# Swapping the two copies of the turned probabilities between ScalarE and VectorE in the prompt attention

## The reference, cut to what matters

```
logits = q @ k^T * scale (+ a bias for fox and swa)
p = softmax(where(mask, logits, -1e30))
out = p @ v
```

## Time and profile before

| | |
|---|---|
| median of 3 runs | 2819.38 us (2811.65 to 2823.92) |
| the profiled execution's own time | 2807.96 us |
| its span, first to last instruction | 2806.0 us |
| mean granted TensorE clock, share of full speed | 0.989 |
| VectorE copies of chunks (L1736) | 144, all of 512 columns |
| ScalarE copies of chunks (L1312) | 144: 60 of 512 columns, 24 of 384, 36 of 256, 24 of 128 |
| first and last start of these copies | 244.8 to 1898.8 us |

### The profile page before, as it was taken

How to read it: one execution, slowest core, us unless ns; L and a number is a source line. 1 busy time by engine, 2 the same in 40 slices (tenths; PEclk the granted TensorE clock), 3 DMA queues, 4 the chain that set the end, 5 groups by cost and what they waited for, 6 DMA issues and landing times.

```text
span 2806.0 us, 39617 instructions
## 1 busy us (share of the span) xinstructions
PE 2695.5 (96%) x14966; PEld 2177.9 (78%) x14966; DVE 1698.6 (61%) x2196; ACT 1054.8 (38%) x1969; POOL 1050.4 (37%) x594
## 2 busy tenths in 40 slices
PE   8999999899999999999999999998999999999997
PEld 6986666787888887888879756667878888878886
DVE  4026777635564558778740377775355564688777
ACT  4225544423323332333332255554243233333333
POOL 1112000114545457767511210001146444667766
PEclk9999999999999999999999999999999999999999
DMA  4212001432333446444132200013413433654441
GB/s 145 63 29 61 25 18 44 137 135 98 124 139 126 150 173 251 142 138 134 61 115 64 66 24 17 17 50 131 163 70 139 157 118 140 238 195 143 143 142 75
DMA packets 164722, 308.75 MB, mean 110 GB/s; under 512 B 24720, under 2 KB 90416, under 8 KB 164592
## 3 DMA queue, kind: packets, MB, share of 16 engines
q1 hardware_dynamic: 161280, 303.59, 31.4%
q10 hardware_dynamic: 3312, 3.41, 0.4%
HBM read 207.40 MB, written 97.72 MB: 109 GB/s over the span
## 4 chain that ended last, share of the span: by engine, by line
PE 86%; DVE 8%; ACT 2%; issue 2%; POOL 1%; DMA 1%; SPq 0%; DVEq 0%; ACTq 0%; POOLq 0%
PE ps L2583 8%; PE ps L2587 8%; PE ps L2585 8%; PE ps L2493 7%; PE ps L2494 7%; PE ps L2495 7%; PE ps L2237 6%; PE ps L2104 6%; PE ps L2106 6%; PE ps L2105 6%; PE ps L2098 5%; PE ps L2310 3%; PE ps L2370 2%; PE ps L2204 1%; PE ps L2438 1%
## 5 line engine op out<-in xcount | busy, mean ns | idle before, releaser
L2583 PE MATMUL ps<-wq_hi,sa_hi 128*128 128x512 f32 x896 | 349.0, 390 | 5.3 <-DVE x L2034 5.3
L2587 PE MATMUL ps<-wq_hi,sa_lo 128*128 128x512 f32 x896 | 348.6, 389 | 0.0
L2585 PE MATMUL ps<-wq_lo,sa_hi 128*128 128x512 f32 x896 | 348.6, 389 | 0.0
L2034 DVE TENSOR_TENSOR x<-ps,x 128x1024 f32<-128x1024 f32 x224 | 266.7, 1215 | 119.5 <-PE ps L2587 115.4
L1082 POOL TENSOR_TENSOR wq_lo<-wsum,wq_hi 128x1024 fp32r<-128x1024 f32 x64 | 157.5, 2462 | 289.7 <-ACT wq_hi L1454 289.7
L1972 DVE TENSOR_TENSOR sa_lo<-ra,sa_hi 128x1024 fp32r<-128x1024 f32 x112 | 253.3, 2263 | 19.8 <-ACT sa_hi L1474 19.7
L2104 PE MATMUL ps<-w_hi,hT_hi 128*128 128x512 f32 (+2 forms) x672 | 248.1, 369 | 0.3 <-DVE hT_lo L1643 0.3
L2106 PE MATMUL ps<-w_hi,hT_lo 128*128 128x512 f32 (+2 forms) x672 | 246.1, 366 | 0.0
L2105 PE MATMUL ps<-w_lo,hT_hi 128*128 128x512 f32 (+2 forms) x672 | 245.1, 365 | 0.0
L1964 DVE TENSOR_TENSOR cq<-ps,cq 128x1024 f32<-128x1024 f32 x48 | 58.6, 1221 | 285.4 <-ACT cq L1515 243.2
L2493 PE MATMUL ps<-hT_hi,wq_hi 128*128 128x512 f32 x512 | 203.2, 397 | 7.6 <-DVE hT_lo L1928 7.6
(11 more groups left out here) (323 smaller groups left out, 6188.1 us busy)
## 6 DMA issues: line engine op xcount, KB each, us to landing
ra<-hidden_scratch SPq DMA_DIRECT2D x112, 512.0 KB, 3.3
hidden_scratch<-cq SPq DMA_DIRECT2D x94, 512.0 KB, 2.7
rq<-in_w_up_dram SPq DMA_DIRECT2D x64, 512.0 KB, 3.9
rq<-in_w_down_dram SPq DMA_DIRECT2D x64, 512.0 KB, 4.3
residual_scratch<-x SPq DMA_DIRECT2D x27, 512.0 KB, 3.1
x<-residual_scratch SPq DMA_DIRECT2D x27, 512.0 KB, 7.3
x<-in_x_prompt_dram SPq DMA_DIRECT2D x16, 512.0 KB, 6.9
w_raw<-in_w_in_dram SPq DMA_DIRECT2D x16, 512.0 KB, 4.2
```

Source lines behind the costliest of these rows:

```text
L2034: nc.vector.tensor_tensor(part, bank(b0 + 2 * pair, 2).rearrange("p (t n) -> p t n", t=2), part, ALU.add).then_inc(dn_ev.sem, 1)
L2583: pe.matmul(out, ah[:, k, :], bh[:, k * 512:(k + 1) * 512], start=new and k == 0, stop=False, skip_group_check=True)
L2585: pe.matmul(out, ah[:, k, :], bl[:, k * 512:(k + 1) * 512], start=False, stop=False, skip_group_check=True)
L2587: last = pe.matmul(out, al[:, k, :], bh[:, k * 512:(k + 1) * 512], start=False, stop=final and k == 1, skip_group_check=True)
```

## The change

ScalarE now copies the chunks with even numbers, out of bank 4, and VectorE those with odd numbers, out of bank 5. The waits of TensorE and the lengths of the two semaphore counts are turned round with them. Nothing else changes: the same copies are made, into the same buffers, at the same places in the two engines' orders.

```diff
-        pt_dve = signal("probsT_copied_dve", (NCHUNK + 1) // 2)
-        pt_act = signal("probsT_copied_act", NCHUNK // 2)
+        pt_act = signal("probsT_copied_act", (NCHUNK + 1) // 2)
+        pt_dve = signal("probsT_copied_dve", NCHUNK // 2)
...
 # ScalarE, attention_step
-                            if ch % 2:
+                            if ch % 2 == 0:
                                 act.wait_ge(pt_mm.sem, pt_mm.at(l, ch + 1))
...
-                                nc.scalar.copy(ptb[ch % NPTB][:, 0:w], bank(5)[:, 0:w]).then_inc(pt_act.sem, 1)
+                                nc.scalar.copy(ptb[ch % NPTB][:, 0:w], bank(4)[:, 0:w]).then_inc(pt_act.sem, 1)
...
 # VectorE, attention_step
-                            if ch % 2 == 0:
+                            if ch % 2:
                                 dve.wait_ge(pt_mm.sem, pt_mm.at(l, ch + 1))
...
-                                nc.vector.tensor_copy(ptb[ch % NPTB][:, 0:w], bank(4)[:, 0:w]).then_inc(pt_dve.sem, 1)
+                                nc.vector.tensor_copy(ptb[ch % NPTB][:, 0:w], bank(5)[:, 0:w]).then_inc(pt_dve.sem, 1)
...
 # TensorE, probs_transposes
-                            done = pt_act if ch % 2 else pt_dve
+                            done = pt_dve if ch % 2 else pt_act
                             pe.wait_ge(done.sem, done.at(l, ch // 2))
...
 # TensorE, values
-                        done = pt_act if ch % 2 else pt_dve
+                        done = pt_dve if ch % 2 else pt_act
                         pe.wait_ge(done.sem, done.at(l, ch // 2 + 1))
```

## The result

The changed kernel takes 2827.52 us (median of 20 runs, 2821.23 to 2836.74), the kernel before, run beside it, 2811.94 us (20 runs). The ratio, which is that of the means (2827.41 to 2813.70), is 1.0049, 95% interval 1.0039 to 1.0059: slower by 11 to 17 us. The profiled execution took 2821.23 us around a span of 2819.3; that of before took 2807.96.

What follows compares the result with a forecast made beforehand. TensorE, busy for 96% of the span, was taken to bound the kernel. Losses of 5.7 less gains of 1.9 make 3.8 us a layer, 7.6 for both; with 1.8 for the clock, 9.4 on 2819.4 gives 2829 us, range 2823 to 2835.

Steps and rivals of the forecast that it cites:

- tile 4, four turnings: VectorE's shorter copy wins 0.30 us at three waits for a normalisation and 0.39 at one, 1.3 a layer.
- tile 5, four turnings: VectorE's shorter copy, less the lag of the second chunk, wins 0.08 us at three turnings and 0.26 at one.
- tile 6: One turning waiting for a normalisation gains 0.13 us a layer; a small loss of 0.1 stands against it.
- window heads, tiles 4, 5, 6: Behind their exponentials ScalarE's now full copy comes late and holds up the turning: +1.3, +1.15, +0.75 us, 3.2 a layer.
- tile 7: Two full chunks: waits of 0.36 and twice 0.1, a turning behind ScalarE's copy 0.24, last product 0.1; 0.9 us a layer.
- tiles 2 and 3: The second chunk's lag costs 0.15 and 0.3 us, a turning behind ScalarE's full copy 0.4; some 0.9 a layer.
- tile 0: The window heads' one chunk moves to VectorE, in front of eight normalisations that a turning waits for: +0.60 us a layer.
- The bound of 0.6 us a layer for the copy of 128 columns: VectorE's unmeasured 128-column copy, priced at 295 ns between 265 and 425; the ends move the sum by under 0.6.
- The clock: At tile 4 two short pauses become one of about 2.1 us; one layer's pause lowers TensorE's clock: +1.8 us.
- A, the freed VectorE: VectorE's shorter copies win: 2797 us if all 21.9 us count, 2816 without the losses; chance 0.12, large form 0.03.
- B: Pauses behind the window heads of tiles 4, 5 and 6 all lower the clock: 18.4 us, 2838, slower by 0.65%; chance 0.18.
- C: No difference, the pauses on both sides being hidden by matmuls: 2819 us; chance 0.15.

Runs made afterwards that it cites:

- after: The changed kernel, the two copies swapped between ScalarE and VectorE in all units, against the kernel before: 2827.52 us, ratio 1.0049.
- after_fill: The changed kernel, with unread turnings by TensorE filling the pauses in front of units 34, 49 and 64: 2823.56 us, 1.0039 to the kernel before.
- swa_only: The kernel before with copies swapped only in units 33, 48 and 63, two steps before the window heads of tiles 4 to 6: 2826.15 us, 1.0047.
- swa_fill: The kernel before with only units 33, 48, 63 swapped, and 20 unread turnings in the pauses before units 34, 49, 64: 2822.66 us, 1.0036.
- swa_back: The changed kernel, but units 33, 48 and 63 keep the copies of the kernel before: 2823.44 us, 1.0045 to the kernel before.
- second_first: The changed kernel, all units swapped, but TensorE turns each unit's second chunk before the first: 2808.70 us, 0.9991 to the kernel before.
- best2: The kernel before, swapped in fox and mla units of tiles 4, 5 without 33, 34, 48, 49, second chunk turned first there: 2805.50 us, 0.9973.
- best: The kernel before with copies swapped in tiles 4 to 6 alone, the second chunk turned first there: 2811.06 us, 0.9991.
- short_only: The kernel before with copies swapped only in fox and mla units of tiles 4 and 5, without 33 and 48: 2810.14 us, 0.9996.
- swa_tile7_back: The changed kernel, but units 33, 48, 63 and those of tile 7 keep their old copies: 2818.59 us, 1.0029 to the kernel before.

## Why the prediction was right, and where not

**The mechanism was right; that the time came so close was luck, for two errors cancel.** Forecast 2829, measured 2827.52. The change itself is 13.8 us (0.0049 x 2812; 15.6 between the medians), not 9.4; and the median it was added to, 2819.38 from three runs, lay 7.4 us above that of the 20 runs. On the later median the same sum would have said 2821.3, 6 us too low, and the forecast's own range, 2816 to 2828, would just have held the measured time.

**The waits: right, step by step.** Shifts per layer, predicted and measured, without the places where the clock differs:

| step | predicted us | measured us |
|---|---|---|
| tile 4, four turnings | -0.30 x 3, -0.39 | -0.31, -0.27, -0.32, -0.40 |
| tile 5, four turnings | -0.08 x 3, -0.26 | -0.09 x 3, -0.27 |
| tile 6 | -0.13 and +0.1 | +0.12, +0.13 |
| window heads, tiles 4, 5, 6 | +1.3, +1.15, +0.75 | +1.30, +1.20, +0.78 |
| tile 7 | +0.9 | +0.84 |
| tiles 2 and 3 | +0.9 | +0.79 |
| tile 0 | +0.60 | +0.42 |
| sum | +3.8 | +3.7 |

The window heads' figures are sums of two units: +1.65 at 34 and -0.35 at 35, since the turning of 34 no longer halts for its fifth block; +1.59 and -0.39; +1.41 and -0.63. One sign of the sum was wrong, the gain at tile 6: there VectorE waits for its chunk and pays the lag in both places. At tile 0 the normalisations come 0.42 later and not 0.60. The bound of 0.6 us a layer for the copy of 128 columns should have been 5 x 0.13 = 0.65; the 288 ns measured make it idle. One expected sign failed: the turning of the window heads of tile 4 was to wait over 0.9 us longer than 0.31, and in after it does not wait: the score matmuls ahead of it run at the lower clock (2.19 us for four, 1.31 before) and cover the wait. In after_fill, where the clock stays up, it waits 0.69. Of the other signs, the waits behind ScalarE's copy (some 5 us a layer forecast, 6.2 measured) stand at the first block of the turning, and ScalarE's busy time grew by 17 us; VectorE's copies take 22 us less as priced (twice the 49.5 of a layer in the earlier trace rows less the 38.5 above), but its busy time fell by 13 and not some 20: the rest of its work took 9 us more, which no term of the sum needed.

**The clock: right in place, too small in size.** The term was "at most what 0.91 leaves out", 1.8 us, for one of the two layers' pauses. It was mis-sized twice. A fall in tile 4 costs 2.6 us when the stretch goes to 0.83, as swa_only against swa_fill shows, and both layers' pauses can have one. And low time grew in places that I gave none, in the profiled execution behind the attention above all; in the mean it grew by 23 us a run. At the 0.37 us that a us of low time costs in the runs of before, these 23 us make 8.6, against the 1.8 of the forecast. The Trainium skill (TensorE: Matmul & The Clock Gate, Terms) reckons with half of the throttled time as the penalty, an estimate of 11.5 us here; the measured 0.37 is less, and it is what I go by. One reason can be seen at units 6 and 8 above, where half of what a fall cost came back in a wait that it covered.

The two parts together give the times. Twice a layer's steps, and 0.37 of the low time over that of before, are in us against the difference of the means from the 99 runs of before: after 7.4 + 8.6 = 16.0 for 15.3 measured, swa_only 7.1 + 6.1 = 13.2 for 12.8, swa_back 3.7 + 9.0 = 12.7 for 12.9, second_first -3.4 + 1.0 = -2.4 for -2.3, best2 -4.9 - 2.1 = -7.0 for -6.9; the other kernels come within 1.2. So swa_back did win back half of the waits, but the clock cost it as much as it cost after; and some 2 us of best2's gain are low time, of which no run shows whether the change or scatter took it away. The 0.37 is read from scatter and not from an experiment of its own.

**The rivals.** A, the freed VectorE, fell: its gains came, 1.8 us a layer, but so did the losses. B had the size nearly (0.65% for a measured 0.49%), but not the mechanism: the pauses at tiles 5 and 6 were 1.65 and 1.15 us, and the clock stayed at 1.00 behind both, in after and in swa_only. The pause of 2.40 us that after has in front of unit 4 in layer 0 had no fall behind it either, where before's 1.98 had one. The pause that best has inside unit 34, 1.69 us in layer 0 and 1.68 in layer 1, went with 1.00 in the first and 0.83 in the second. So B's threshold between 1.0 and 1.5 us isn't there, and a length alone doesn't decide. C was wrong: nothing was hidden.

**What stays open.** Why swa_back, whose longer pauses are the 0.69 at units 35 and 50, 2.40 for 1.98 at tile 0 and 1.64 for 1.30 at 505 us, had as much low time as after, and where the half of after's extra low time that filling its three pauses left comes from. The parts that ran by themselves had none of it; tile 6 didn't run alone.

## What to carry to other kernels

When two engines share the copies of a ring of banks, the engine whose queue holds long work just there must not hold the bank that is wanted first; find the steps where its copy starts late, and swap around them. Giving the freed engine its short chunk first took the loss away (0.9991); doing so only in the steps with short chunks, and leaving out those around the window heads, gave a small gain (0.9973). And time a change of half a per cent against runs of the kernel before from the same series: three runs put the base 7 us off, as much as the waits that were to be predicted.

## What the runs showed of the hardware

- A copy of 128 columns, fp32, from PSUM by VectorE takes 288 ns, of 256, 384 and 512 columns 422, 555 and 689: 133 ns for each 128, and some 155 besides.
- One pause of TensorE of 2.16 us in dense work is followed by the lower clock in both layers of after and of swa_only, and twenty turnings of a block in it keep the clock at 1.00. Pauses of 1.65 and 1.15 us weren't followed by it, nor was one of 2.40 us at tile 0 in layer 0 of after. A pause of 1.7 us in best, and three of 0.5, 0.7 and 0.7 us close together in swa_back and short_only, were in layer 1 and not in layer 0; the same three were in both layers of swa_tile7_back. In after the same pause cost 0.7 us in one layer and 2.0 in the other by the shift at units 35 and 36. The Trainium skill (TensorE: Matmul & The Clock Gate, Part 1) says that the chip's watch on TensorE runs free and doesn't start with the kernel; that the same pause is answered differently in two layers fits this, and no run here tests it.
- In the profiled executions where filling had prevented a fall at one pause, later falls were longer: from 480 to 560 us the shift grew by 4.1 us in swa_fill for 1.3 in swa_only. With one execution of each, it isn't shown that the one made the other. What counts is the low time of the whole run, which between versions that differ in a few steps went from 57 to 89 us, and each us of it goes with 0.37 us of time.
